# A transformer trunk on one core: the prologue reordered around one late mean, the first bias made by TensorE, later means from two rounded parts, and leading tiles in three pairs of steps

## The reference

```
def rmsnorm(x, g):                     # six of them
    y = x * rsqrt(mean(x * x, over features) + 1e-6);  return y * g

proj = rmsnorm(x, norm_pre) @ w_in     # q | k | v | z (1024 columns each) | f (16 columns)
c = cumsum(log_sigmoid(f + b_f), over tokens)
logit[t, s] = q_t . k_s / 8 + c[t] - c[s]   for s <= t, else -inf;  softmax over s;  @ v
x = x + rmsnorm((o * silu(z)) @ w_out, norm_post)
x = x + sigmoid(rmsnorm(x, pe_norm) @ pe_w_gate) * (p @ pe_w_proj)
```

## Time and profile before

| | us |
|---|---|
| median of 3 runs | 641.18 (640.65 to 641.36) |
| profiled execution, its own time | 641.69 |
| its span | 639.9 |
| PE busy | 629.9 (98%) |
| DVE, ACT, POOL busy | 385.4, 324.1, 298.8 |

### The profile page before, as it was taken

The page is one execution under the profiler, slowest core; times in us unless marked ns, Lnnn a source line. Parts: engine busy times, 40 slices in busy tenths (PEclk is TensorE's granted clock), DMA queues, the critical chain, the costliest instruction groups (busy, mean ns, idle before and its releaser), DMA issues.

```text
span 639.9 us, 9274 instructions
## 1 busy us (share of the span) xinstructions
PE 629.9 (98%) x2928; PEld 516.4 (81%) x2928; DVE 385.4 (60%) x776; ACT 324.1 (51%) x559; POOL 298.8 (47%) x404
## 2 busy tenths in 40 slices
PE   7999999999999999999999999999999999999997
PEld 4788888888888888888788778888888888887886
DVE  5558786787868687555969635342434243367764
ACT  7738575665657576465656532231222222466451
POOL 1776554636455455200447458546554742002470
PEclk8999999999999999999999999999999999999999
DMA  5354333433333334044102314333223232242031
GB/s 205 97 188 140 108 107 108 127 119 115 115 117 117 126 120 112 34 164 166 33 18 102 112 67 131 98 98 105 91 85 112 98 131 69 97 164 98 1 132 67
DMA packets 27161, 68.69 MB, mean 107 GB/s; under 512 B 3568, under 2 KB 10096, under 8 KB 27136
## 3 DMA queue, kind: packets, MB, share of 16 engines
q1 hardware_dynamic: 27136, 68.37, 32.4%
HBM read 66.23 MB, written 2.13 MB: 107 GB/s over the span
## 4 chain that ended last, share of the span: by engine, by line
PE 91%; POOL 3%; issue 2%; DVE 1%; ACT 1%; DMA 1%; SPq 0%; POOLq 0%; DVEq 0%
PE ps_pj L1033 25%; PE ps_pj L1035 25%; PE ps_pj L1034 25%; PE ps_tr L1042 3%; POOL w_lo L410 2%; PE ps_o L1143 2%; PE ps_o L1142 2%; PE ps_sc L1112 1%; PE ps_tr L1033 1%; PE ps_tr L1035 1%; PE ps_tr L1034 1%; PE ps_sc L1110 1%; PE ps_o L1067 1%; PE ps_o L1048 1%; DMA xT<-in_xT 1%
## 5 line engine op out<-in xcount | busy, mean ns | idle before, releaser
L410 POOL TENSOR_TENSOR w_lo<-w_raw,w_hi 128x256 fp32r<-128x256 f32 x316 | 241.1, 796 | 132.7 <-ACT w_hi L468 132.7
L1033 PE MATMUL ps_pj<-act_hi,w_hi 128*128 128x512 f32 (+1 forms) x728 | 288.9, 397 | 1.0 <-issue 0.2
L1035 PE MATMUL ps_pj<-act_hi,w_lo 128*128 128x512 f32 (+1 forms) x728 | 282.6, 388 | 0.0
L1034 PE MATMUL ps_pj<-act_lo,w_hi 128*128 128x512 f32 (+1 forms) x728 | 282.2, 388 | 0.0
L1033 PEld LDWEIGHTS ps_pj<-act_hi,w_hi 128*128 128x128 f32 x728 | 136.9, 188 | 29.2 <-issue 4.8
L1035 PEld LDWEIGHTS ps_pj<-act_hi,w_lo 128*128 128x128 f32 x728 | 136.7, 188 | 28.6
L1034 PEld LDWEIGHTS ps_pj<-act_lo,w_hi 128*128 128x128 f32 x728 | 137.0, 188 | 24.8 <-issue 0.7
L468 ACT CAST w_hi<-w_raw 128x1024 fp32r<-128x1024 f32 x96 | 100.6, 1048 | 88.9 <-DMA w_raw<-in_weights 66.7
L445 POOL TENSOR_TENSOR acc<-acc,sq 128x512 f32<-128x512 f32 x14 | 22.5, 1604 | 116.1 <-ACT sq L616 115.8
L418 POOL TENSOR_TENSOR bias<-bias,future 128x128 f32<-128x128 f32 x64 | 33.9, 561 | 73.2 <-DMA bias<-negc_scratch 73.2
L523 ACT ACTIVATE logit<-logit,nmax 128x128 f32<-128x128 f32 (+1 forms) x64 | 36.0, 563 | 44.7 <-DVE nmax L764 44.5
(11 more groups left out here) (142 smaller groups left out, 746.7 us busy)
## 6 DMA issues: line engine op xcount, KB each, us to landing
w_raw<-in_weights SPq DMA_DIRECT2D x100, 512.0 KB, 3.3
bias<-negc_scratch SPq DMA_DIRECT2D x16, 256.0 KB, 7.3
bias<-negc_scratch SPq DMA_DIRECT2D x16, 192.0 KB, 6.2
xT<-in_xT SPq DMA_DIRECT2D x8, 256.0 KB, 4.3
bias<-negc_scratch SPq DMA_DIRECT2D x16, 128.0 KB, 4.8
out<-xT SPq DMA_DIRECT2D x7, 256.0 KB, 2.2
bias<-negc_scratch SPq DMA_DIRECT2D x16, 64.0 KB, 3.6
p_in<-in_pT SPq DMA_DIRECT2D x2, 512.0 KB, 4.5
```

Of the source, the lines that this page charges most:

```text
L410: last = nc.gpsimd.tensor_tensor(w_lo[place % RING][:, tiles], w_raw[stream(place) % RAW][:, tiles], w_hi[place % RING][:, tiles], ALU.sub ...
L1033: nc.tensor.matmul(out, w_h, a[0][:, k, tokens], start=k == first, stop=False)
L1034: nc.tensor.matmul(out, w_h, a[1][:, k, tokens], start=False, stop=False)
L1035: end = nc.tensor.matmul(out, w_l, a[0][:, k, tokens], start=False, stop=k == last)
```

## The change

1. **x and q together.** SP loads slot 0 behind the first tile of x and slot 1 behind the last. DVE rounds slot 0 (ACT did). PE runs the hi*hi and lo*hi matmuls of q for each tile of x as it comes, right behind the forget gate's, then those of k (slot 1), then one mean, then the hi*lo matmuls of both.
2. **One late mean.** ACT squares tiles 0 to 3 among the tiles and 4 to 7 after them, seven of them into PSUM banks, DVE adds them all into one tile (`x_acc`), and one float32 matmul takes the place of four.
3. **The first bias by PE.** For head 0 the running sum isn't loaded from DRAM: a float32 matmul with row 0 of `mean_f` brings it to 128 partitions (`ps_negc`), and DVE multiplies by 1024 and adds a mask of 512 columns (`first_bias`). Head 1's is still loaded; SP issues it ahead of slot 4. Turn 0 is written out by hand on PE, with hi*hi and lo*hi first and hi*lo after. `scale(1)` moves ahead of the running sum on DVE.
4. **Two-part means.** For norms 2, 3 and 5, ACT rounds `acc` (`acc_round`), DVE takes the rest (`acc_rest`), and PE does two fp32r matmuls (`split_mean`) in place of one float32. Norms 1 and 4 stay.
5. **Leading tiles.** In the pairs of steps at `STEP_CONV` and at the second `STEP_OUT`, the first step runs one tile ahead of the second (`lead`).

The core of the diff:

```diff
@@ block.sync
                 if k == 0:
                     sp.dma_start(g_pre[:], pre_in).then_inc(g_loaded[0], 16)
                     sp.dma_start(f_raw[:], f_in).then_inc(f_loaded, 16)
+                    load_slot(0, 0)
+            load_slot(1, 1)
             sp.dma_start(b_f[:], b_f_in).then_inc(g_loaded[1], 16)
-            for slot in range(4):
-                load_slot(slot, slot)
+            load_slot(2, 2)
+            load_slot(3, 3)
             sp.wait_ge(f_chain, 1)
             sp.dma_start(negc_dram, f_negc[:]).then_inc(negc_stored, 16)
             sp.wait_ge(negc_stored, 16)
+            load_bias(0, 1)
             load_slot(4, 4)
-            load_bias(0, 0)
             load_slot(5, 5)
             load_slot(6, 6)
-            load_bias(0, 1)
@@ block.gpsimd (slots 0 to 2 ahead, then)
-            with pool.Fori(0, PAIRS) as m:
+            for slot in range(3, 6):
+                weight_lo(slot, slot)
+            mask_rows(0, 1)
+            weight_lo(6, 6)
+            with pool.Fori(1, PAIRS) as m:
                 turn(m)
@@ block.scalar
-                nc.scalar.activation(x_sq[k][:], xT[:, k, :], ACT.Square).then_inc(x_sq_act, 1)
-            weight_hi(0, 0)
+                for n in SQUARES_AT.get(k, []):
+                    x_square(n)
+            act.wait_ge(w_hi_done, 1)
+            weight_hi(1, 1)
+            for n in range(4, KT):
+                x_square(n)
...
+            def acc_round(n):
+                act.wait_ge(acc_done, KT * n)
+                nc.scalar.copy(acc_hi[:], acc[:]).then_inc(acc_hi_done, 1)
...
             norm_scale(0, rs[:])
-            weight_hi(1, 1)
+            weight_hi(2, 2)
@@ block.vector
+                if k == 0:
+                    dve.wait_ge(w_loaded[0], 16)
+                    nc.vector.tensor_copy(w_hi[0][:], w_raw[0][:]).then_inc(w_hi_done, 1)
+                for n in SUMS_AT.get(k, []):
+                    dve.wait_ge(x_sq_act, n + 1)
+                    wait(dve, x_sum, n - 1)
+                    nc.vector.tensor_tensor(x_acc[:], ps_square[(n - 1) % SQUARE_BANKS][:], x_acc[:], ALU.add
+                                            ).then_inc(x_sum, 1)
...
+            def first_bias():
+                dve.wait_ge(consts, 5)
+                dve.wait_ge(negc_wide, 1)
+                for i in range(TT):
+                    n = (i + 1) * P
+                    nc.vector.scalar_tensor_tensor(bias[0][:, i, 0:n], ps_negc[:, 0:n], float(D), mask[:, SEQ - n:SEQ],
+                                                   ALU.mult, ALU.add).then_inc(bias_ready[0], 1)
...
+            def acc_rest(n):
+                dve.wait_ge(acc_hi_done, n)
+                nc.vector.tensor_tensor(acc_lo[:], acc[:], acc_hi[:], ALU.subtract).then_inc(acc_lo_done, 1)
@@ block.tensor
+            def split_mean(n):
+                pe.wait_ge(mean_rounded, 1)
+                pe.wait_ge(acc_lo_done, n)
+                nc.tensor.matmul(ps_o[:], mean_r[:], acc_hi[:], start=True, stop=False)
+                nc.tensor.matmul(ps_o[:], mean_r[:], acc_lo[:], start=False, stop=True).then_inc(ms_done, 1)
...
+                first_hi(0, [k])
+            first_hi(1, range(KT))
+            pe.wait_ge(x_sum, KT - 1)
+            nc.tensor.matmul(ps_o[:], mean_f[:], x_acc[:], start=True, stop=True).then_inc(ms_done, 1)
+            first_lo(0)
+            first_lo(1)
+            pe.wait_ge(pj_free[0], 1)
+            first_hi(2, range(KT))
+            pe.wait_ge(f_chain, 1)
+            nc.tensor.matmul(ps_negc[:], mean_f[0:1, :], f_negc[0:1, :], start=True, stop=True).then_inc(negc_wide, 1)
+            first_lo(2)
+            pe.wait_ge(pj_free[1], 1)
+            first_hi(3, range(KT))
+            pe.wait_ge(pj_free[0], 2)
+            transposes(USE_V, [scaled[0][:, t * P:(t + 1) * P] for t in range(TT)])
+            first_lo(3)
...
-            turn(0, 0, True, False)
             turn(1, 0, True, True)
...
-                norm_mean(3 * l + 2)
+                split_mean(2 * l + 1)
...
                     side_by_side(STEP_CONV, SLOT_CONV, act1, ACT_H[1],
-                                 between={KT - 3: lambda: norm_mean(3)})
+                                 between={KT - 3: lambda: split_mean(2)}, lead=True)
```

More of the change, by code:

```diff
@@ L163, in trunk @@
         f_negc = f_abs
-        x_sq = [sb(f"x_sq{k}", [P, SEQ], at=f_part) for k in range(KT)]
+        x_acc = sb("x_acc", [P, SEQ], at=f_part)
         f_part.close()
@@ L183, in trunk @@
         rs2 = sb("rs2", [P, SEQ], at=late)
+        acc_hi = sb("acc_hi", [P, SEQ], F32R, late)
+        acc_lo = sb("acc_lo", [P, SEQ], F32R, late)
         g_raw = [sb(f"g_raw{i}", [P, SEQ], at=late) for i in range(2)]
@@ L478, in log_exp_tables, with x_square @@
                 nc.scalar.preload_act_table_set("natural_log_exp_and_others")
+            def x_square(n):
+                out = x_acc if n == 0 else ps_square[(n - 1) % SQUARE_BANKS]
+                wait(act, x_sum, n - SQUARE_BANKS)
+                nc.scalar.activation(out[:], xT[:, n, :], ACT.Square).then_inc(x_sq_act, 1)
             log_exp_tables()
@@ L602, in _ @@
             turn(PAIRS, 0, False, True)
+            act.wait_ge(consts, 3)
+            nc.scalar.copy(mean_r[:], mean_f[:]).then_inc(mean_rounded, 1)
             def square(n, src):
@@ L724, in _ @@
         def _(dve):
-            added = 0
             for k in range(KT):
@@ L803, in turn @@
                         scale(0)
-                    if g == 8 and project:
+                    if g == 4 and not attend:
+                        scale(1)
+                        forget_sums()
+                    if g == 11 and not attend:
+                        first_bias()
+                    if g == 8 and project and attend:
                         scale(1)
@@ L1168, in step, with side_by_side, part @@
                     end.then_inc(pj_done, 1)
-            def side_by_side(s, slot, a, tiles, wide=False, between={}, from_k=0):
-                for k in range(from_k, KT):
-                    pe.wait_ge(act_ready, tiles + k + 1)
-                    for j in range(2):
-                        if j == 1 and k in between:
-                            between[k]()
-                        if k == 0:
-                            weights_ready(slot + j)
-                            pe.wait_ge(pj_free[(s + j) % 2], (s + j) // 2)
-                        end = products(ps_pj[(s + j) % 2], slot + j, a, [k], 0, KT - 1)
-                        if k == KT - 1:
-                            end.then_inc(pj_done, 1)
+            def side_by_side(s, slot, a, tiles, wide=False, between={}, from_k=0, lead=False):
+                def part(k, j):
+                    pe.wait_ge(act_ready, tiles + k + 1)
+                    if j == 1 and k in between:
+                        between[k]()
+                    if k == 0:
+                        weights_ready(slot + j)
+                        pe.wait_ge(pj_free[(s + j) % 2], (s + j) // 2)
+                    end = products(ps_pj[(s + j) % 2], slot + j, a, [k], 0, KT - 1)
+                    if k == KT - 1:
+                        end.then_inc(pj_done, 1)
+                if lead:
+                    part(from_k, 0)
+                for k in range(from_k, KT):
+                    if not lead:
+                        part(k, 0)
+                    elif k < KT - 1:
+                        part(k + 1, 0)
+                    part(k, 1)
                     if wide:
```

84 lines of the change are left out of this document (44 added, 40 removed).

## The result

| | us |
|---|---|
| before, median of 9 runs beside the kernel after | 640.91 (639.08 to 642.83) |
| after, median of 9 runs | 644.54 (642.85 to 648.43) |
| ratio after / before | 1.005, 95% interval 1.0031 to 1.007 |
| profiled execution after, its span | 644.54, 642.5 |

What follows compares the result with a forecast made beforehand. PE, busy 98% of the span, was taken to bound the kernel. Terms -1.2 - 1.1 + 1.1 + 1.6 - 0.6 = -0.2 us on 641.18 gave 641.0 us, range 639.1 to 642.9.

Steps and rivals of the forecast that it cites:

- Prologue steps, slot 4, turn 1's start: Prologue to turn 1: slot 4 lands at 37.5 behind the bias, PE begins products at 41.6, not 40.50: +1.1 us.
- The low clock: Start of turn 1, after PE's 5.6 us wait: 1.2 GHz for some 3.2 us of PE's work, +1.6 us.
- the inside of turn 1: Turn 1: PE's hole at 51.14 closes because PE is over 2 us later, -0.6 us.
- The base of the sum: Whole kernel: profiled 641.69 lies 0.5 above the median of the runs, so -0.2 us is applied to 641.18.
- Later means and leading tiles: Norms 2, 3, 5: -0.41 us a mean, -1.2 in all; pairs of steps: three holes of 0.36 covered, -1.1 us.
- the low clock comes in the x stage too: Rival, x stage: 1.2 GHz there as well makes everything 1 to 1.5 us later, 642.0 to 642.5; chance 0.15.
- slot 4 passes the bias: Rival, prologue: slot 4 isn't held up, lands at 33.5, PE begins at 37.6: -5.2 us, 636.0; chance 0.10.
- the clock stays high: Rival, turn 1: no low clock after the wait and the hole only moves: -1.2 us, 640.0; chance 0.18.
- the split parts come late: Rival, later norms: each mean waits for ACT and DVE, parts 4 and 5 give 1.5, not 2.3: 641.8; chance 0.05.

Runs made afterwards that it cites:

- the ten matmuls more: Kernel before with split means and leading tiles, plus two 128x512 matmuls behind each of the first five forget products: 638.26 us, ratio 0.9964.
- the 18 matmuls more: Changed kernel with 18 more 128x512 matmuls behind turn 1's first score, where PE waits for slot 4: 643.73 us, ratio 1.0046.
- the one with all turns swapped: Kernel before with head 1's bias issued behind the third weight slot instead of ahead, in all seven turns with bias loads: 659.09 us, ratio 1.0282.

## Why the prediction was wrong

The sum can now be made over profiles. Eight with the old prologue (seven as it was, one with the ten matmuls more) have the first score of turn 2 at 68.48 to 70.94, mean 69.78; the four with the new one and slot 4 behind the bias at 73.64 to 74.78, mean 74.06 (the one with the 18 matmuls more left out); the four with slot 4 ahead, three of them edited further, 68.21 to 70.03, mean 69.19. Turn 8 takes 54.2 (the same eight, with the run of the kernel before that had slot 4 behind the bias in place of the one with all turns swapped), 55.1 and 54.8 us. The later parts give 2.1. The 0.25 us outside the span comes on top, and is rounded to +0.2.

| | turn 2 | turn 8 | later | outside the span | sum | by the times |
|---|---|---|---|---|---|---|
| after | +4.3 | +0.9 | -2.1 | +0.2 | +3.3 | +3.2 |
| after with slot 4 ahead | -0.6 | +0.6 | -2.1 | +0.2 | -1.9 | -1.6 to -2.4 |

- *Prologue steps, slot 4, turn 1's start*: the wait and what releases it were right, 41.92 for 41.6. That the number fits so well is partly luck: the bias went out 1.0 us sooner than forecast (27.31 for 28.3), and from there slot 4 took 10.6 us to land, the figure of before without the 1.3 that I took off it. That this order is the cause is shown from both sides, in the kernel after (-5.5 us) and in the kernel before (+9).
- *The low clock and the inside of turn 1*: the low clock came, for over 4 us in place of 3.2. Its price beyond what was slack is about 1 us or less, so the +1.6 was too much. The -0.6 for the hole at 51.14 was wrong as well: from turn 1's products to turn 2 it takes 31.7 us for 30.4 before (29.6 to 30.5 over the eight with the old prologue), and 30.7 with the 18 matmuls more and the full clock. So without the low clock this stretch is about as long as it was, and not 0.6 shorter. PE is 2.7 us later at turn 2 in this pair (1.4 at turn 1's products, 1.3 behind them), for +1.1 +1.6 -0.6 = +2.1.
- *The base of the sum*, and this is the step that failed with the most us: "Against the profiled execution's 641.69 ... so the forecast is 641.18 - 0.2". I compared the new prologue with the 40.50 of one execution, whose x stage had run at 0.50, and took the 0.5 by which that execution lay over the median off both kernels. Three of the eight profiles with the old prologue are like it (granted clock 0.50 to 0.55 in the x stage, turn 2 at 70.5 to 70.9), five are not (1.00, 68.5 to 69.9). The new prologue is not to be compared with 70.92 but with 69.8. That alone is 1.1 us of the 3.4 that are missing. How much it is exactly stays open: it hangs on how often the stage falls, 3 times in 8 profiles, and by the 134 timed executions the 641.69 lies 1.4 over their median, 640.26. I had the rows in front of me, used them for the clock of turn 1 and as a danger for the new x stage, and never asked what before would be without them.
- *The same on the other side.* The first profile of after has the fastest x stage of the four. ACT took the second tile at 7.16 there, and at 7.93, 8.04 and 7.38 in the others, at 5.6 to 6.0 in the old order (6.8 once): with slot 0 ahead of it this tile is later, and scattered. It makes another 0.4 us.
- *Left out*: turn 8, 0.9 us, the second largest part. The forecast took it that a lateness is carried unchanged to the end. For turns 2 to 7 that is right to 0.01 us; turn 8 has no projection, its scores stand closer, and all nine profiles with any form of the new prologue take more there (54.5 to 56.3) than is usual with the old one (54.1 to 54.3, once 54.6). In one profile it was the late bias; why it is so on the whole is open. The 0.2 outside the span was left out too, and its cause is open.
- *Later means and leading tiles*: -2.1 for -2.3. The lead was sized too small (1.4 for 1.1), the split too large (0.6 for 1.2): its -0.41 a mean is right, but two holes in the steps behind the means of norms 2 and 5 grew by 0.5 together.
- *Rivals.* That the low clock comes in the x stage too was seen in two of nine profiles of the new prologue, none of them of the kernel after. That slot 4 passes the bias is refuted: 8.8 us against 3.1 when it is issued first. That the clock stays high did not happen either, and that the split parts come late shows nowhere: no mean waits.

The terms add up: 1.1 (the old x stage) + 0.4 (the new one) + 0.6 (turn 1's start and inside) + 0.9 (turn 8) + 0.2 (later parts) + 0.2 (outside the span) = 3.4, and a forecast of -0.2 was +3.2 when measured. That they meet this closely is partly luck, as the measured 3.2 is known to 1.2 us either way.

Two versions are faster than both kernels: the later parts in the old prologue (0.9963), and the whole change with slot 4 ahead (0.9963). They can't be told apart, so the new prologue, once mended, shows no gain over the old; these intervals would not show one below about 1 us.

## What to carry to other kernels

Before a profile is used as the sum's base, look whether its own stretches hold something that another execution may not have (here a granted clock of 0.50 for 3.4 us), and ask what the base would be without it; if the change touches that stretch, it belongs to the sum. A load that the next stage waits for goes ahead of transfers that have time: two lines were worth 5.5 us here, more than all the rest of the change. And a hole that closes is often a hole that moves: the busy PE in the wait for slot 4 and the bias behind v's scaling each closed one and opened another.

## Not expected of the hardware

- The same stretch of the kernel before, with PE busy 1.67 and 1.68 of 3.30 us ahead of it, ran at 1.00 in one execution and at 0.50 in another, with the same instructions. In this case whether PE's clock falls there is not fixed by the program. The Trainium skill ("TensorE: Matmul & The Clock Gate", Part 1, on the HAM clock gate) says that the hardware watches PE's activity in windows that run free of the program. By that rule one stretch of work can fall either way, and the two executions agree.
- Four transfers of head 1's bias ahead of one of 512 KB made it land 8.8 us after its issue, for 3.1 without them, though they are 640 KB together. Even at the pace of that load (512 KB in 3.1 us, so 3.9 for 640 KB) this would be an estimate of 7.0 us: more than their size alone explains. What in them is slow was not tested.
